# The conditioning vectors of a two-block network: column products on VectorE, ScalarE and GpSimd, and sums over partitions on TensorE

## The chip, the cores and the metric

The kernel runs on one core of a Trainium2 chip. A core has five engines with queues of their own: TensorE (matrix multiplication), VectorE, ScalarE, GpSimd, and SyncE, which here only issues DMAs. The metric is the device time of one execution in microseconds, the median of several runs.

## The reference

Two blocks are computed for a sequence x of 256 rows and 1024 columns, all in fp32. The first block has two layers of retention with stick-breaking attention and a gated feed-forward. The second block has two layers of feed-forward, mixer, feed-forward, for x and for a context of 256 rows. Its norms are modulated by nine vectors of 1024 in each layer, for x from c and for the context from c_ctx:

```python
sc, scc = jax.nn.silu(c), jax.nn.silu(c_ctx)
for l in range(DEPTH):                                   # 2
    mod_x = (sc @ w_mod[l] + b_mod[l]).reshape(b_, N_MOD, 1, D_MODEL)    # N_MOD = 9
    mod_h = (scc @ w_mod[l] + b_mod[l]).reshape(N_MOD, 1, D_MODEL)
    ...
# adaln_in:  rmsnorm(s, g_pre) * (1 + scale) + shift
# adaln_out: s + weight * gate * rmsnorm(y, g_post)
```

So w_mod is 2 x 1024 x 9216, 75 MB, and is multiplied by two vectors only. The last layer uses the context only up to its keys and values, so the last chunks of its w_mod are wanted for x alone.

## The kernel before

The work is a list of ten sub-layers, 0 to 9 (plan, SUBS): retention, feed-forward, retention, feed-forward of the first block, then feed-forward, mixer, feed-forward, twice. Each has a wide phase (input matrices, in chunks of 512 columns; a feed-forward has 11 chunks, each of 256 gate and 256 up columns) and a tall phase (output matrix). Weights come in units of 128x1024 fp32, 524 in all, over a ring of four slots (RING): SyncE loads raw, ScalarE rounds it to whi (split_hi, line 1102), VectorE takes the rest, wlo (split_lo, line 1663), and TensorE does three matmuls for each product (hi by hi, hi by lo, lo by hi). SyncE loads a unit when the unit four before it has been split; ScalarE copies a unit when the unit four before it has been used (unit_done of the trailing pass).

A wide chunk is four units. In the sub-layers with two row tiles (0 to 3 and 9) each unit holds 2 of the 8 blocks of the contraction; TensorE runs over the four units with the first tile (the leading pass) and then over the four with the second (the trailing pass), six matmuls a unit and pass. After the second unit of a leading pass it transposes hrow of the chunk before (gate_transposes for the trailing tile), after the second of a trailing pass that of the leading tile. VectorE's program for one chunk is: hrow of the chunk before, trailing tile; hrow of this chunk, leading tile; four splits for the next chunk. ScalarE's is sgate and hid for the tiles and the four copies, in the same order. With four row tiles (4 to 8), the chunks after the first of a feed-forward are computed transposed in one pass (wide_across), 24 matmuls a unit.

The modulation is laid between these passes by a plan made when the kernel is built (mod_plan). The 36 column chunks of w_mod make nine groups of four. A group has eight steps, one for each block of 128 rows (mod_step, inside the pe program): a load of 1 MB into mraw (two slots), and four matmuls of 512 columns, one for each chunk, whose stationary side is cstat, 32 columns of which the first two are silu(c) and silu(c_ctx); they lie in four column groups of the array and add up in PSUM bank 2. A step follows every second unit's trailing pass, in sub-layers 1, 3, 4, 6 (two groups each) and 7 (one). VectorE then copies the bank to mrow, TensorE turns it to columns with sel, and VectorE adds b_mod into modT.

GpSimd does the inverse roots, the rotary products and the DMAs of the gain rows (gain_rows, into grow). During the wide phases of the sub-layers with modulation it has nothing to do.

Of the kernel before, what the change touches and what calls it, by code (L numbers as in the profile page):

```python
# [152 lines left out]
def mod_plan():  # L153


    after, rows_at, cols_at = {}, {}, {}
    g = 0
    for i, groups in ((1, 2), (3, 2), (4, 2), (6, 2), (7, 1)):
        for j in range(groups):
            first = SUBS[i]["u_wide"] + 4 + 16 * j  # L160
            for k in range(KD):
                after[first + 2 * k] = KD * g + k
            rows_at[first + 14], cols_at[first + 18] = g, g
            g += 1
    return after, rows_at, cols_at


QUADS_AFTER, ROWS_AT, COLS_AT = mod_plan()
N_QUADS = len(QUADS_AFTER)
QUAD_UNIT = {q: u for u, q in QUADS_AFTER.items()}  # L170
assert N_QUADS == 2 * MOD_CHUNKS * DEPTH
N_Q4 = 48


def weight_units():
# [60 lines left out]
def build(nc, a, out):  # L236
    ctx = ExitStack()
    with ctx:  # L238
# [60 lines left out]
        r_row = region("grow", 8192)  # L299
        grow = at("grow", [P, 2, D], F32, r_row)  # L300
        rmask = at("rmask", [P, 4, 384], F32, r_row)
        cs1 = at("cs1", [P, 2, 2, P], F32, r_row + 6144)

        ident = sb("ident", [P, P])
# [10 lines left out]
        cT = sb("cT", [P, KD, 2])  # L315
        mrow = sb("mrow", [P, CH])
        sel = sb("sel", [P, 8])
        cstat = sb("cstat", [P, KD, 32])
# [42 lines left out]
        mraw_landed = [sem(f"mraw_landed{i}") for i in range(2)]  # L361
        ws_landed = sem("ws_landed")
        vgain_landed = sem("vgain_landed")
        out_landed = sem("out_landed")
# [2 lines left out]
        a_split = sem("a_split")  # L367
        w_split = sem("w_split")
        unit_done = sem("unit_done")
        mod_used = sem("mod_used")  # L370
        mod_rows = sem("mod_rows")
        mod_cols = sem("mod_cols")
        mod_taken = sem("mod_taken")
# [141 lines left out]
        @block.sync  # L515
        def _(sp):
            def load_main(u, slot, first=False):
                if not first:
                    sp.wait_ge(w_split, u - RING + 1)
                sp.dma_start(raw[:, slot, :], a["w"][WEIGHTS[u]]).then_inc(raw_landed[slot], 16)  # L520

            def load_mod(q):
                if q >= 2:
                    sp.wait_ge(mod_used, q - 1)
                g, k = q // KD, q % KD
                chunks = a["w_mod"].rearrange("(c u) p n -> c u p n", u=4)[4 * g:4 * g + 4, k // 2]
                src = chunks[:, :, CH * (k % 2):CH * (k % 2) + CH].rearrange("c p n -> p c n")
                sp.dma_start(mraw[:, q % 2, :, :], src).then_inc(mraw_landed[q % 2], 16)

            def load_mods(u):  # L530
                after_mix = SUBS[6]["u_wide"] + 4
                if u == after_mix:

                    sp.wait_ge(a_split, SUBS[6]["a0"])
                    load_mod(N_Q4)
                    load_mod(N_Q4 + 1)
                for q in range(2, N_QUADS):
                    if q not in (N_Q4, N_Q4 + 1) and QUAD_UNIT[q - 2] + 2 * RING == u:
                        load_mod(q)
# [12 lines left out]
            load_main(1, 1, first=True)  # L552
            load_x(1)
            load_main(2, 2, first=True)
            load_main(3, 3, first=True)
            for name, dst in (("cT", cT), ("lam", lamw), ("sink", sink)):
                constant(name, dst, small_landed, name != "cT")
            for u in range(RING, N_UNITS):
                load_main(u, u % RING)
                if u in LATE_AT:  # L560
                    name, dst = LATE_AT[u]
                    constant(name, dst, late_landed)
                if u in BLOCK2_AT:
# [4 lines left out]
                if u in (26, 27):  # L568
# [14 lines left out]
        def _(pe):  # L583
# [28 lines left out]
                        if i == nt - 1 and k % per == per - 1:  # L612
                            ins.then_inc(tr_ready, 1)

            def mod_step(q):
                g, k = q // KD, q % KD
                pe.wait_ge(mraw_landed[q % 2], 16 * (q // 2 + 1))
                if q == 0:
                    pe.wait_ge(c_split, 1)
                if k == 0 and g:  # L620
                    pe.wait_ge(mod_rows, g)
                for j in range(4):
                    last = mm(ps[32 * j:32 * j + 32, 2 * BANK:3 * BANK], cstat[:, k, :], mraw[:, q % 2, j, :],
                              k == 0, k == KD - 1)
                last.then_inc(mod_used, 1)

            def mod_columns(g):
                pe.wait_ge(mod_rows, g + 1)
# [4 lines left out]
                last.then_inc(mod_cols, 1)  # L633

            def modulation(u):
                if u in QUADS_AFTER:
                    mod_step(QUADS_AFTER[u])
                if u in COLS_AT:
                    mod_columns(COLS_AT[u])

# [447 lines left out]
        def _(act):  # L1088
# [563 lines left out]
        def _(dve):  # L1652
# [7 lines left out]
            def split_lo(u):  # L1660
                slot = u % RING
                dve.wait_ge(hi_done, u + 1)
                nc.vector.tensor_tensor(wlo[:, slot, :], raw[:, slot, :], whi[:, slot, :].bitcast(F32),  # L1663
                                        ALU.subtract).then_inc(w_split, 1)
                modulation(u - RING - 1)

            def mod_rows_out(g):
                dve.wait_ge(mod_used, KD * (g + 1))
# [12 lines left out]
                last.then_inc(mod_taken, 1)  # L1681

            def modulation(u):
                if u in ROWS_AT:
                    mod_rows_out(ROWS_AT[u])
                if u in COLS_AT:
                    mod_out(COLS_AT[u])

# [679 lines left out]


            dve.sem_inc(gate_done, LEAD4)  # L2370
            nc.vector.memset(cstat[:, :, :], 0.0).then_inc(dve_link, 1)
            n["link"] += 1
# [11 lines left out]
            nc.vector.tensor_copy(cstat[:, :, 0:2], cT[:, :, :])  # L2384
# [27 lines left out]
        def _(pool):  # L2412
# [16 lines left out]
            def gain_rows(s):  # L2429
# [16 lines left out]
                for st in range(streams):  # L2446
                    pool.dma_start(grow[:, st, :], gains[st].partition_broadcast(P)).then_inc(grow_ready, 16)

            def rope(view, cos, tmp, swap):

                t1, t2 = tmp
# [50 lines left out]
                inverse_roots(SUBS[0]["wide"][st])  # L2502
            for i, s in enumerate(SUBS):
                nxt = SUBS[i + 1] if i + 1 < len(SUBS) else None
                gain_rows(s)
                if s["kind"] == "ret":
                    rope_first(s)
                    for i0 in (8, 0):
                        inverse_roots_of_heads(i0, i0 + 8)
                if s["kind"] == "mix":  # L2510
                    pool.wait_ge(mod_used, N_Q4 if s["l"] == 0 else N_QUADS)
# [129 lines left out]
```

## Time and profile before

| | |
|---|---|
| time, median of 3 runs | 2510.45 us (2509.3 to 2510.86) |
| the profiled execution | 2511.7 us, span 2509.5 us |
| TensorE (PE) busy | 2418.1 us, 96% |
| VectorE (DVE) busy | 1144.3 us, 46% |
| ScalarE (ACT) busy | 1021.5 us, 41% |
| GpSimd (POOL) busy | 164.2 us, 7% |
| mean granted TensorE clock | 0.987 |
| moved by DMA | 364.34 MB, mean 145 GB/s |

The span runs from the first to the last instruction of the profiled execution; what its own time has beyond it lies before and after. Matmuls are pipelined and their ends are modelled, so that a difference of starts says what one costs, and the sum of durations does not. The times of sub-layer 1 (units 36 to 101) are about 140 to 360 us of the span, those of sub-layer 3 about 490 to 705, of sub-layer 9 from 2300 on.

### The profile page before, as it was taken

To read this page: it belongs to the slowest core of one execution; us is meant where nothing else is said; L and a number is where in the kernel's file an instruction comes from. 1 tells how busy PE (TensorE), PEld (TensorE's weight loads), DVE (VectorE), ACT (ScalarE), POOL (GpSimd) and SP (SyncE) were. 2 spreads that over 40 slices of the span, in tenths; PEclk is the share of its full clock that TensorE was granted. 3 is DMA by queue.
4 is the path that set the end of the run, shared out by engine and by line. 5 is a ranking of instruction groups with operands and counts; after the bars stand their busy time and mean duration, and the time that the engine had idled before them with its cause. 6 is when DMAs were issued, how large, how long until landed. Compare 5 with 4: busy or idle time off the path is not lost. (4 is left out here: it accounts for less than half of the span.)

```text
span 2509.5 us, 29213 instructions
## 1 busy us (share of the span) xinstructions
PE 2418.1 (96%) x11296; PEld 1902.9 (76%) x11296; DVE 1144.3 (46%) x1900; ACT 1021.5 (41%) x1766; POOL 164.2 (7%) x205
## 2 busy tenths in 40 slices
PE   8999999999999999999989999999999999997998
PEld 6776777766877778877677777887778887766777
DVE  5654455644552223363656222335323335456455
ACT  6443446543542222354545222234322234445444
POOL 1200003000010000013001000000000000310000
PEclk9999999999999999999989999999999999999999
DMA  6558654478545532323103554322442222322554
GB/s 212 188 185 293 236 175 164 138 261 292 194 138 185 175 134 91 103 69 125 43 26 109 193 176 168 109 85 92 161 142 93 100 86 92 115 70 76 181 187 143
DMA packets 118728, 364.34 MB, mean 145 GB/s; under 512 B 11072, under 2 KB 11712, under 8 KB 118592
## 3 DMA queue, kind: packets, MB, share of 16 engines
q1 hardware_dynamic: 116336, 355.62, 41.2%
q0 software_dynamic: 2256, 6.86, 0.9%
q8 instruction: 91, 1.49, 0.2%
q14 instruction: 45, 0.37, 0.1%
HBM read 361.35 MB, written 1.09 MB: 144 GB/s over the span
## 5 line engine op out<-in xcount | busy, mean ns | idle before, releaser
L1663 DVE TENSOR_TENSOR wlo<-raw,whi 128x1024 fp32r<-128x1024 f32 x524 | 644.2, 1234 | 732.4 <-ACT whi L1102 728.3
L1102 ACT CAST whi<-raw 128x1024 fp32r<-128x1024 f32 x524 | 548.2, 1050 | 618.2 <-PE ps L588 607.9
L588 PE MATMUL ps<-whi,xhi 128*128 128x512 f32 x1136 | 470.3, 414 | 25.9 <-ACT fbuf L1132 14.3
L588 PE MATMUL ps<-whi,xlo 128*128 128x512 f32 x1136 | 449.9, 396 | 0.0
L588 PE MATMUL ps<-wlo,xhi 128*128 128x512 f32 x1136 | 448.8, 395 | 0.0
L588 PE MATMUL ps<-whi,ahi 128*128 128x512 f32 x952 | 374.5, 393 | 7.6 <-DVE alo L1924 5.0
L588 PE MATMUL ps<-xhi,whi 128*128 128x512 f32 x960 | 378.9, 395 | 0.0
L588 PE MATMUL ps<-xhi,wlo 128*128 128x512 f32 x960 | 373.8, 389 | 0.0
L588 PE MATMUL ps<-xlo,whi 128*128 128x512 f32 x960 | 373.6, 389 | 0.0
L588 PE MATMUL ps<-whi,alo 128*128 128x512 f32 x952 | 371.8, 391 | 0.0
L588 PE MATMUL ps<-wlo,ahi 128*128 128x512 f32 x952 | 371.6, 390 | 0.0
L588 PEld LDWEIGHTS ps<-whi,xhi 128*128 128x128 f32 x1136 | 217.6, 192 | 99.3 <-issue 46.5
L588 PEld LDWEIGHTS ps<-whi,xlo 128*128 128x128 f32 x1136 | 216.7, 191 | 48.7
L588 PEld LDWEIGHTS ps<-wlo,xhi 128*128 128x128 f32 x1136 | 218.1, 192 | 39.3
L588 PEld LDWEIGHTS ps<-xhi,whi 128*128 128x128 f32 x960 | 180.2, 188 | 67.6 <-issue 31.9
L588 PEld LDWEIGHTS ps<-whi,ahi 128*128 128x128 f32 x952 | 179.4, 188 | 47.0 <-ACT proj L1330 4.8
L588 PEld LDWEIGHTS ps<-xhi,wlo 128*128 128x128 f32 x960 | 180.2, 188 | 38.3
L588 PEld LDWEIGHTS ps<-whi,alo 128*128 128x128 f32 x952 | 179.4, 188 | 37.9
L588 PEld LDWEIGHTS ps<-xlo,whi 128*128 128x128 f32 x960 | 180.3, 188 | 36.0
L588 PEld LDWEIGHTS ps<-wlo,ahi 128*128 128x128 f32 x952 | 179.7, 189 | 36.4
L1116 ACT CAST ahi<-hid 128x128 fp32r<-128x128 f32 (+1 forms) x264 | 86.4, 350 | 203.7 <-PE ps L588 203.6
L2423 POOL TENSOR_TENSOR rstd<-ms,mhalf 128x1 f32<-128x1 f32 (+1 forms) x55 | 38.7, 704 | 1946.4 <-DVE ms L1824 1319.5
(163 smaller groups left out, 1660.8 us busy)
## 6 DMA issues: line engine op xcount, KB each, us to landing
raw<-in_w SPq DMA_DIRECT2D x524, 512.0 KB, 3.4
mraw<-in_w_mod SPq DMA_DIRECT2D x72, 1024.0 KB, 6.6
grow<-gains POOLq DMA_DIRECT2D x11, 512.0 KB, 5.8
x<-in_x SPq DMA_DIRECT2D x2, 512.0 KB, 5.2
x<-in_ctx SPq DMA_DIRECT2D x1, 1024.0 KB, 7.7
out<-x SPq DMA_DIRECT2D x2, 512.0 KB, 2.6
rmask<-in_rmask SPq DMA_DIRECT2D x1, 768.0 KB, 5.2
ws<-in_ws POOLq DMA_DIRECT2D x2, 256.0 KB, 7.4
```

What stands on the lines that cost most here:

```text
L588: return nc.tensor.matmul(o, lhsT, rhs, start=start, stop=stop, skip_group_check=True)
L1102: nc.scalar.copy(whi[:, slot, :], raw[:, slot, :]).then_inc(hi_done, 1)
L1116: nc.scalar.copy(ahi[:, w * aslot:w * aslot + w], src[:, row, P * tiles[0]:P * tiles[0] + w]).then_inc(a_hi_done, 1)
L1663: nc.vector.tensor_tensor(wlo[:, slot, :], raw[:, slot, :], whi[:, slot, :].bitcast(F32), ALU.subtract).then_inc(w_split, 1)
L2423: nc.gpsimd.tensor_tensor(rstd[:, m0:m], ms[:, m0:m], mhalf[:, m0:m], ALU.pow).then_inc(rstd_ready, 1)
```

## The change

The modulation's products leave TensorE. A piece is now two column chunks of one block of rows (128 x 2 x 512, 0.5 MB), 144 in all; mraw has four slots of that size. A group is 16 pieces, one behind each of the 16 units from the seventh of its stretch on, and not one step behind every second unit.

- VectorE, for x: after split_lo(u) it multiplies the piece by silu(c), one value per partition, and adds it to macc in one scalar_tensor_tensor; the first piece of a half of a group is written by tensor_scalar.
- ScalarE, for the context, 112 of the 144: after split_hi(u) it multiplies the same piece by silu(c_ctx) with an activation, into msc1 or msc2 (two halves); the first two of a group go straight to macc.
- GpSimd, for the context: mod_group adds each scaled piece to macc, 14 for each of seven groups, 98 in all. The calls stand ahead of gain_rows in GpSimd's program.
- TensorE: mod_sum, once for each group, waits for all its pieces and additions and sums macc over the partitions, with a column of ones as the stationary side; 8 matmuls where there is a context part, else 4. It stands after the trailing pass of unit 18 (or 34) of the sub-layer; the group's last piece goes with unit 21 (37).
- SyncE loads a piece when the one four before it has been used by VectorE and ScalarE.

macc lies in rows, msc1 behind the operands of the first block, msc2 in grow. Copies to mrow, the turn to columns and modT are as they were.

```diff
-        for j in range(groups):
-            first = SUBS[i]["u_wide"] + 4 + 16 * j
-            for k in range(KD):
-                after[first + 2 * k] = KD * g + k
-            rows_at[first + 14], cols_at[first + 18] = g, g
+        for j in range(groups):
+            first = SUBS[i]["u_wide"] + 16 * j
+            pieces += [first + 6 + p for p in range(2 * KD)]
+            sum_at[first + 18], cols_at[first + 22] = g, g
...
+N_P4 = 96
+N_CTX = 112
...
-        mraw = at("mraw", [P, 2, 4, CH], F32, r_m)
+        mraw = at("mraw", [P, 4, 2, CH], F32, r_m)
+        macc = at("macc", [P, 2, 4, CH], F32, places["rows"])
...
+        ADDED = 2 * KD - 2
+        def scaled_pieces(s):
+            return msc1 if s["blk"] == 1 else msc2
...                                                        # sync
-            def load_mod(q):
-                if q >= 2:
-                    sp.wait_ge(mod_used, q - 1)
+            def load_mod(p):
+                if p >= 4:
+                    sp.wait_ge(mod_x, p - 3)
+                    sp.wait_ge(mod_scaled, min(p - 3, N_CTX))
...
+                    if p not in range(N_P4, N_P4 + 4) and PIECE_UNIT[p - 4] + RING + 2 == u:
+                        load_mod(p)
...                                                        # tensor
-            def mod_step(q):
-                g, k = q // KD, q % KD
-                pe.wait_ge(mraw_landed[q % 2], 16 * (q // 2 + 1))
...
-                for j in range(4):
-                    last = mm(ps[32 * j:32 * j + 32, 2 * BANK:3 * BANK], cstat[:, k, :], mraw[:, q % 2, j, :],
-                              k == 0, k == KD - 1)
-                last.then_inc(mod_used, 1)
+            def mod_sum(g):
+                parts = 2 if 2 * KD * g < N_CTX else 1
+                pe.wait_ge(mod_x, 2 * KD * (g + 1))
+                if parts == 2:
+                    pe.wait_ge(mod_ctx, ADDED * (g + 1))
...
+                for i in range(parts):
+                    for j in range(4):
+                        last = mm(ps[32 * j:32 * j + 32, 2 * BANK:3 * BANK], unit_col[:, i, :], macc[:, i, j, :],
+                                  i == 0, i == parts - 1)
+                last.then_inc(mod_summed, 1)
...                                                        # scalar, in split_hi(u)
+                if u in PIECE_AFTER:
+                    mod_piece(PIECE_AFTER[u], u)
+            def mod_piece(p, u):
+                if p >= N_CTX:
+                    return
+                s = [s for s in SUBS if s["u_wide"] <= u][-1]
+                g, k, half = p // (2 * KD), p % (2 * KD) // 2, p % 2
+                act.wait_ge(mraw_landed[p % 4], 16 * (p // 4 + 1))
+                act.wait_ge(c_silu, 1)
+                if k == 0:
+                    if g:
+                        act.wait_ge(mod_summed, g)
+                    dst = macc[:, 1, 2 * half:2 * half + 2, :]
+                else:
+                    if k >= 2:
+                        act.wait_ge(mod_ctx, ADDED * g + 2 * k - 3 + half)
+                    elif g:
+                        act.wait_ge(mod_ctx, ADDED * g)
+                    dst = scaled_pieces(s)[:, half, :, :]
+                nc.scalar.activation(dst, mraw[:, p % 4, :, :], ACT.Copy, scale=cT[:, k, 1:2]).then_inc(mod_scaled, 1)
...                                                        # vector, in split_lo(u)
+                if u in PIECE_AFTER:
+                    mod_piece(PIECE_AFTER[u])
+            def mod_piece(p):
+                g, k, half = p // (2 * KD), p % (2 * KD) // 2, p % 2
+                dve.wait_ge(mraw_landed[p % 4], 16 * (p // 4 + 1))
+                acc, piece = macc[:, 0, 2 * half:2 * half + 2, :], mraw[:, p % 4, :, :]
+                if k == 0:
+                    if g:
+                        dve.wait_ge(mod_summed, g)
+                    nc.vector.tensor_scalar(acc, piece, cT[:, k, 0:1], None, ALU.mult).then_inc(mod_x, 1)
+                else:
+                    dve.wait_ge(mod_x, p - 1)
+                    nc.vector.scalar_tensor_tensor(acc, piece, cT[:, k, 0:1], acc, ALU.mult, ALU.add).then_inc(mod_x, 1)
...                                                        # gpsimd, ahead of gain_rows(s)
+                for g in MOD_SUBS.get(i, ()):
+                    mod_group(s, g)
+            def mod_group(s, g):
+                if 2 * KD * g >= N_CTX:
+                    return
+                for p in range(2 * KD * g + 2, 2 * KD * (g + 1)):
+                    half = p % 2
+                    n["mod"] += 1
+                    pool.wait_ge(mod_scaled, p + 1)
+                    if p >= 2 * KD * g + 4:
+                        pool.wait_ge(mod_ctx, n["mod"] - 2)
+                    acc = macc[:, 1, 2 * half:2 * half + 2, :]
+                    nc.gpsimd.tensor_tensor(acc, acc, scaled_pieces(s)[:, half, :, :], ALU.add).then_inc(mod_ctx, 1)
+                pool.wait_ge(mod_ctx, n["mod"])
```

## Rows read from the trace of the kernel before

**Rows 1.** The page: busy time, share of the span, instructions.

```profile
PE 2418.1 (96%) x11296; PEld 1902.9 (76%) x11296; DVE 1144.3 (46%) x1900; ACT 1021.5 (41%) x1766; POOL 164.2 (7%) x205
```

**Rows 2.** Instructions with mraw: duration ns min/median/max, first and last start.

```profile
L588 PE MATMUL ps<-mraw,cstat x576: 592/605/617, 167.5 to 1864.5; 128*32 128x512 f32 x192
```

**Rows 3.** Timeline (start us, us, ...), TensorE, sub-layer 1, around a step.

```profile
164.72 0.39 PE L588 MATMUL ps<-whi,xhi 128*128 128x512 f32 x1
...
167.22 0.39 PE L588 MATMUL ps<-whi,xlo 128*128 128x512 f32 x1
167.53 1.06 PE L588 MATMUL ps<-mraw,cstat 128*32 128x512 f32 x8
168.53 0.50 PE L588 MATMUL ps<-whi,xhi 128*128 128x512 f32 x1
```

**Rows 4.** Timeline, ScalarE, sub-layer 9: first copies of two chunks.

```profile
2321.55 1.05 ACT L1102 CAST whi<-raw 128x1024 fp32r<-128x1024 f32 x1 [0.39 <-PE ps L588]
...
2333.20 1.05 ACT L1102 CAST whi<-raw 128x1024 fp32r<-128x1024 f32 x1 [0.98 <-PE ps L588]
```

**Rows 5.** Timeline, ScalarE, sub-layer 1: copies of units 40, 51 and 76.

```profile
155.94 1.05 ACT L1102 CAST whi<-raw 128x1024 fp32r<-128x1024 f32 x1 [0.89 <-PE ps L588]
...
188.58 1.05 ACT L1102 CAST whi<-raw 128x1024 fp32r<-128x1024 f32 x1 [1.55 <-PE ps L588]
...
283.13 1.06 ACT L1102 CAST whi<-raw 128x1024 fp32r<-128x1024 f32 x1 [0.88 <-PE ps L588]
```

**Rows 6.** Timeline, VectorE, sub-layer 1: the end of one burst.

```profile
189.67 1.23 DVE L1663 TENSOR_TENSOR wlo<-raw,whi 128x1024 fp32r<-128x1024 f32 x1 [1.38 <-ACT whi L1102]
190.81 0.47 DVE L1912 SCALAR_TENSOR_TENSOR hrow<-ps,rstd,sgate 128x256 f32<-128x256 f32 x1
```

**Rows 7.** Timeline, TensorE, at the same place.

```profile
190.90 0.39 PE L588 MATMUL ps<-whi,xlo 128*128 128x512 f32 x1
191.34 0.44 PE L647 MATMUL ps<-ident,hrow 128*128 128x128 f32 x2
```

**Rows 8.** Two lines of VectorE, columns as in rows 2.

```profile
L1832 DVE SCALAR_TENSOR_TENSOR x<-rows,rstd,x x20: 1276/1280/1286, 1089.3 to 2505.2; 128x1024 f32<-128x1024 f32 x20
L1704 DVE TENSOR_SCALAR rows<-x,rstd x22: 743/753/755, 705.5 to 2314.0; 128x1024 f32<-128x1024 f32 x22
```

**Rows 9.** Groups of ScalarE: count, busy us, mean ns, idle before, releasers.

```profile
L1197 ACT ACTIVATE rows<-x 128x1024 f32<-128x1024 f32 x32 | 33.9, 1059 | 45.1 <-DVE x L1804 24.4 <-DVE x L1832 16.6 <-DMA x<-in_x 2.4
...
L1285 ACT COPY hid<-ps 128x256 f32<-128x256 f32 x78 | 28.2, 370 | 95.9 <-PE ps L647 95.9
```

**Rows 10.** Timeline, GpSimd, sub-layer 0 (rotary products).

```profile
62.65 1.48 POOL L2456 TENSOR_TENSOR proj<-rope 128x512 f32<-128x512 f32 x1
67.06 1.56 POOL L2452 TENSOR_TENSOR rope<-proj,cs 128x512 f32<-128x512 f32 x1 [2.93 <-ACT proj L1330]
...
71.05 1.27 POOL L2456 TENSOR_TENSOR proj<-rope 128x512 f32<-128x512 f32 x1
...
73.87 1.42 POOL L2454 TENSOR_TENSOR rope<-proj,cs 128x256 f32<-128x256 f32 x2
```

**Rows 11.** Timeline, VectorE, sub-layer 0, at the same time.

```profile
62.91 2.30 DVE L1663 TENSOR_TENSOR wlo<-raw,whi 128x1024 fp32r<-128x1024 f32 x1
...
67.40 2.30 DVE L1663 TENSOR_TENSOR wlo<-raw,whi 128x1024 fp32r<-128x1024 f32 x1
...
69.63 1.01 DVE L2027 TENSOR_TENSOR zs<-zs,ps 128x384 f32<-128x384 f32 x2
```

**Rows 12.** Stretches: busy us (count) of PE, PEld, DVE, ACT, POOL; PEclk, DMA share, GB/s.

```profile
735.00:919.90 184.90, 184.90 (x865) 139.28 (x864) 50.29 (x53) 42.69 (x52) 1.10 (x2) 1.00 0.51 176
181.80:195.90 14.10, 14.05 (x72) 9.38 (x73) 5.78 (x6) 5.67 (x8) 0.00 (x0) 1.00 0.83 295
```

**Rows 13.** Timeline, TensorE, end of sub-layer 4, after idleness.

```profile
1107.13 0.47 PE L588 MATMUL ps<-whi,xhi 128*128 128x512 f32 x1 [3.28 <-ACT fbuf L1132]
```

**Rows 14.** A stretch there, columns as in rows 12.

```profile
1107.00:1112.00 5.00, 4.87 (x14) 3.87 (x15) 5.00 (x9) 2.26 (x6) 1.25 (x1) 0.66 0.47 156
```

More of the change, by code:

```diff
@@ L153, in mod_plan @@
 def mod_plan():
-    after, rows_at, cols_at = {}, {}, {}
+    subs, pieces, sum_at, cols_at = {}, [], {}, {}
     g = 0
     for i, groups in ((1, 2), (3, 2), (4, 2), (6, 2), (7, 1)):
+        subs[i] = range(g, g + groups)
         for j in range(groups):
-            first = SUBS[i]["u_wide"] + 4 + 16 * j
-            for k in range(KD):
-                after[first + 2 * k] = KD * g + k
-            rows_at[first + 14], cols_at[first + 18] = g, g
+            first = SUBS[i]["u_wide"] + 16 * j
+            pieces += [first + 6 + p for p in range(2 * KD)]
+            sum_at[first + 18], cols_at[first + 22] = g, g
             g += 1
[L165 to L172, printed above, removed]
+    return subs, pieces, sum_at, cols_at
+MOD_SUBS, PIECE_UNIT, SUM_AT, COLS_AT = mod_plan()
+N_PIECES = len(PIECE_UNIT)
+PIECE_AFTER = {u: p for p, u in enumerate(PIECE_UNIT)}
+assert N_PIECES == 4 * MOD_CHUNKS * DEPTH == len(PIECE_AFTER)
+N_P4 = 96
+N_CTX = 112
 def weight_units():
@@ L301, in build @@
         rmask = at("rmask", [P, 4, 384], F32, r_row)
+        msc1 = at("msc1", [P, 2, 2, CH], F32, r_x + 16384)
+        msc2 = at("msc2", [P, 2, 2, CH], F32, r_row)
         cs1 = at("cs1", [P, 2, 2, P], F32, r_row + 6144)
@@ L317, in build @@
         sel = sb("sel", [P, 8])
-        cstat = sb("cstat", [P, KD, 32])
+        unit_col = sb("unit_col", [P, 2, 32])
         modT = sb("modT", [P, DEPTH, N_MOD * KD, 2])
@@ L360, in build @@
         raw_landed = [sem(f"raw_landed{i}") for i in range(RING)]
-        mraw_landed = [sem(f"mraw_landed{i}") for i in range(2)]
+        mraw_landed = [sem(f"mraw_landed{i}") for i in range(4)]
         ws_landed = sem("ws_landed")
@@ L369, in build @@
         unit_done = sem("unit_done")
-        mod_used = sem("mod_used")
+        mod_x = sem("mod_x")
+        mod_scaled = sem("mod_scaled")
+        mod_ctx = sem("mod_ctx")
+        mod_summed = sem("mod_summed")
         mod_rows = sem("mod_rows")
@@ L520, in load_main @@
                 sp.dma_start(raw[:, slot, :], a["w"][WEIGHTS[u]]).then_inc(raw_landed[slot], 16)
-            def load_mod(q):
-                if q >= 2:
-                    sp.wait_ge(mod_used, q - 1)
-                g, k = q // KD, q % KD
-                chunks = a["w_mod"].rearrange("(c u) p n -> c u p n", u=4)[4 * g:4 * g + 4, k // 2]
+            def load_mod(p):
[3 more added lines that the diff above has]
+                g, k, half = p // (2 * KD), p % (2 * KD) // 2, p % 2
+                c0 = 4 * g + 2 * half
+                chunks = a["w_mod"].rearrange("(c u) p n -> c u p n", u=4)[c0:c0 + 2, k // 2]
                 src = chunks[:, :, CH * (k % 2):CH * (k % 2) + CH].rearrange("c p n -> p c n")
-                sp.dma_start(mraw[:, q % 2, :, :], src).then_inc(mraw_landed[q % 2], 16)
+                sp.dma_start(mraw[:, p % 4, :, :], src).then_inc(mraw_landed[p % 4], 16)
             def load_mods(u):
-                after_mix = SUBS[6]["u_wide"] + 4
-                if u == after_mix:
+                if u == SUBS[6]["u_wide"] + 4:
                     sp.wait_ge(a_split, SUBS[6]["a0"])
[L535 to L539, printed above, removed]
+                    for p in range(N_P4, N_P4 + 4):
+                        load_mod(p)
+                for p in range(4, N_PIECES):
+                    if p not in range(N_P4, N_P4 + 4) and PIECE_UNIT[p - 4] + RING + 2 == u:
+                        load_mod(p)
             def constant(name, dst, sem_, broadcast=False):
@@ L567, in _ @@
                     sp.dma_start(x[:, 2:4, :], a["ctx"].rearrange("b (t p) d -> p (b t) d", p=P)).then_inc(block2_landed, 16)
-                if u in (26, 27):
+                if u in (26, 27, 28, 29):
                     load_mod(u - 26)
@@ L613, in transposes_in @@
                             ins.then_inc(tr_ready, 1)
-            def mod_step(q):
-                g, k = q // KD, q % KD
-                pe.wait_ge(mraw_landed[q % 2], 16 * (q // 2 + 1))
-                if q == 0:
+            def mod_sum(g):
[3 more added lines that the diff above has]
+                    pe.wait_ge(mod_ctx, ADDED * (g + 1))
+                if g == 0:
                     pe.wait_ge(c_split, 1)
-                if k == 0 and g:
+                else:
                     pe.wait_ge(mod_rows, g)
-                for j in range(4):
-                    last = mm(ps[32 * j:32 * j + 32, 2 * BANK:3 * BANK], cstat[:, k, :], mraw[:, q % 2, j, :],
-                              k == 0, k == KD - 1)
-                last.then_inc(mod_used, 1)
+                for i in range(parts):
[3 more added lines that the diff above has]
+                last.then_inc(mod_summed, 1)
             def mod_columns(g):
@@ L635, in modulation @@
             def modulation(u):
-                if u in QUADS_AFTER:
-                    mod_step(QUADS_AFTER[u])
+                if u in SUM_AT:
+                    mod_sum(SUM_AT[u])
                 if u in COLS_AT:
@@ L1665, in split_lo @@
                 modulation(u - RING - 1)
+                if u in PIECE_AFTER:
+                    mod_piece(PIECE_AFTER[u])
+            def mod_piece(p):
+                g, k, half = p // (2 * KD), p % (2 * KD) // 2, p % 2
+                dve.wait_ge(mraw_landed[p % 4], 16 * (p // 4 + 1))
[4 more added lines that the diff above has]
+                    nc.vector.tensor_scalar(acc, piece, cT[:, k, 0:1], None, ALU.mult).then_inc(mod_x, 1)
+                else:
+                    dve.wait_ge(mod_x, p - 1)
+                    nc.vector.scalar_tensor_tensor(acc, piece, cT[:, k, 0:1], acc, ALU.mult, ALU.add).then_inc(mod_x, 1)
             def mod_rows_out(g):
-                dve.wait_ge(mod_used, KD * (g + 1))
+                dve.wait_ge(mod_summed, g + 1)
                 if g:
@@ L1683, in modulation @@
             def modulation(u):
-                if u in ROWS_AT:
-                    mod_rows_out(ROWS_AT[u])
+                if u in SUM_AT:
+                    mod_rows_out(SUM_AT[u])
                 if u in COLS_AT:
@@ L2370, in _ @@
             dve.sem_inc(gate_done, LEAD4)
-            nc.vector.memset(cstat[:, :, :], 0.0).then_inc(dve_link, 1)
-            n["link"] += 1
+            link(nc.vector.memset(unit_col[:, :, :], 0.0))
+            for i in range(2):
+                nc.vector.memset(unit_col[:, i, i:i + 1], 1.0)
             nc.vector.memset(ones[:, :], 1.0)
@@ L2383, in _ @@
             dve.wait_ge(c_silu, 1)
-            nc.vector.tensor_copy(cstat[:, :, 0:2], cT[:, :, :])
             nc.vector.tensor_copy(sel[:, :].rearrange("p (j t) -> p j t", j=4),
@@ L2510, in _ @@
                 if s["kind"] == "mix":
-                    pool.wait_ge(mod_used, N_Q4 if s["l"] == 0 else N_QUADS)
+                    pool.wait_ge(mod_x, N_P4 if s["l"] == 0 else N_PIECES)
                     pool.dma_start(ws[:, :, :], a["ws"][s["l"]]).then_inc(ws_landed, 16)
```

## The prediction

> **What bounds the kernel now.** I read the page first. TensorE is busy in 96% of the span of 2509.5 us [rows 1], and the chain of waits is nearly all its matmuls. So a microsecond leaves the total only where TensorE itself gets it back, and a microsecond on another engine counts where TensorE comes to wait for it. Next I asked for the instructions that read mraw, and for TensorE's timeline around one of them: what does the modulation cost TensorE? Then the chunk cycle of a two-tile gate/up phase (sub-layers 1, 3 and 9), by ScalarE's, VectorE's and TensorE's timelines: how much room have the two engines that the change loads? Last, all places where VectorE and GpSimd work at once.
>
> Modulation today: 576 records of 605 ns [rows 2], 8 to a step, 72 steps, overlapping. In the timeline the last matmul of the unit starts at 167.22 and the next unit's first at 168.53 [rows 3]. From 164.72 on, matmuls of weights start 0.227 us apart (eleven steps to 167.22), so a step costs 1.31 - 0.23 = 1.08 us of TensorE, and 72 steps 78 us.
>
> **Two-tile chunk cycle (sub-layers 1 and 3).** A ring slot is held from the leading to the trailing pass. A pass of one unit is 6 x 0.227 = 1.36 us. ScalarE may copy a unit of the next chunk when the trailing pass of the same-numbered unit of this one ends. From first copy to first copy a chunk takes 2333.20 - 2321.55 = 11.65 us in sub-layer 9, which has no modulation [rows 4]. In sub-layer 1 the nine chunks from 155.94 to 283.13 take 127.2 us [rows 5]; sub-layer 3 is the same stretch again. The rows to look at are the end of the burst. VectorE's program is: four splits, then hrow of the chunk before (trailing tile). TensorE wants that hrow after the *second* leading pass. Slot 3 comes free at 188.58 [rows 5], its split runs 189.67 to 190.90, hrow 190.81 to 191.28 [rows 6], and TensorE, done with the second leading pass, transposes hrow at 191.34 [rows 7]. There is no slack: whatever is put on VectorE between the splits and hrow delays TensorE.
>
> **Part 1, matmuls out, sums in.** Out: 72 x 1.08 = 78. In: seven groups sum two parts and two groups one, 16 sums of the form of a step, 16 x 1.08 = 17. TensorE's own gain is 61 us. Column sums, copies of rows and modT stay.
>
> **Part 2, VectorE.** One piece of 128x1024 behind each of 144 splits. The nearest rows are a scalar_tensor_tensor of that size at 1.28 and, for the first of a group, tensor_scalar at 0.75 [rows 8]; queued behind each other some 0.08 is hidden, as between split and hrow [rows 6]. **ScalarE** gets 112 scalings, near the 1.05 of its copy [rows 5]; other 1024-wide activations take 1.06 [rows 9].
>
> **Part 3, GpSimd.** 98 additions of 128x1024. The trace has 512 wide at 1.27 and two of 256 at 1.42, so 0.71 each [rows 10]: slope 2.19 ns per element, 1.27 + 512 x 0.00219 = 2.39 us. Bounds: 2.2 (slope alone) and 2 x 1.56 = 3.1 (from the longest row shown). By the Trainium skill (GPSIMD Engine Reference, Elementwise — side-by-side cycle accounting) a two-input add of 2048 takes 4497 ns; half is, as an estimate, 2.25, which would take 0.14 off each of the 56 additions that count below, 8 us.
>
> **Part 4, what the two do to each other.** GpSimd's 512-wide multiplication at 62.65 ends at 64.13, and VectorE's split, issued at 62.91, takes 2.30 instead of 1.23: 1.22 of waiting and 1.08 of work. The same at 67.06 (ends 68.62) and 67.40 [rows 10, 11]. At 69.63 two operations with one input in PSUM and one in SBUF take 1.01, no longer than usual, beside GpSimd [rows 11]. So operations with two SBUF inputs take turns with GpSimd, whole instructions at a time, and both the split and the new piece are of that kind. The Trainium skill (SBUF — State Buffer, SBUF: two separate sides) calls it an exclusive lock on a port pair and gives it to whichever starts first, for the whole instruction; it promises no turns, and by it alone VectorE could keep the pair through its queue, which is rival A. In turns VectorE holds it 1.08 and GpSimd about 2.28 (2.39 less what it dispatches meanwhile; for 512 it would be 64.13 - 62.99 = 1.14).
>
> *Full chunk* (four pieces, four additions; six of them in each of sub-layers 1 and 3). Time 0 is the first copy. ScalarE: copy 0 to 1.05, scale 2.1, copy 3.15, scale 4.2, then hid 0.37 [rows 9], copy 5.6, scale 6.65, copy 7.7, scale 8.9. From 1.1 on there is always something to add, so the holders are four splits, four pieces and four additions: 8 x 1.08 + 4 x 2.28 = 17.8, done at 19.0. hrow to 19.5, transposes to 19.95, third and fourth leading pass 2.72, trailing pass 1.36: 24.05 us instead of 11.65.
> *Chunk 1*: its pieces 6 and 7 open a group (0.75 each, no addition): two such behind the last two splits, 13.2.
> *Chunks 5 and 9*, where a group is summed: TensorE asks for the sum after the third trailing pass (4.1), but needs the pieces and additions of units whose slots came free at 0 and 1.36: 1.1 + 4 x 1.08 + 2 x 2.28 = 10.0. Sum 2.15, to 12.2; fourth trailing pass 13.6; only now the last copy, split, row copy 0.68, piece and hrow, 17.6; transposes, two leading passes and one trailing: 22.1, in chunk 9 (no pieces for 38 and 39) 21.5.
> Nine chunks: 13.2 + 6 x 24.05 + 22.1 + 21.5 = 201.1 against 127.2: +73.9, in both sub-layers **+148**.
>
> *Four-tile sub-layers 4, 6, 7.* 32 units take 184.9 us with modulation, 5.78 each, 5.45 the 24 matmuls alone; VectorE is busy 50.3 of it, 1.57 a unit [rows 12], and with a piece and a wait for an addition gets 1.08 + 2.28 more: 4.9. A unit may be copied four units ahead. The cover holds. TensorE gets back 40 x 1.08 - 8 x 1.08 = 34.6; at each of the three sums with additions it waits some 0.3 to 0.5 (copy, split, addition and piece after one another take 5.8 of the 5.45 it has). **-33**.
>
> *TensorE's clock.* In a full chunk TensorE now idles some 9 us before hrow. After 3.28 us of idleness it restarts at 1107.13 [rows 13], and in 1107 to 1112 the granted clock is 0.66, part at 1.2 instead of 2.4 GHz [rows 14]: 5 x 0.34 = 1.7 us lost. The passes behind hrow are on the path. Sixteen chunks (all but the first of each nine): **+27**. Bounds: nothing, and all 4.1 us of the exposed passes at half clock, 66 us.
>
> SP: pieces of half the size, one a unit, the same bytes. Share of the DMA engines in such a chunk was 0.83 at 14.1 us [rows 12]; at 24 it falls. GpSimd's gain_rows now queue behind the additions, but they serve the end of the tall phase, over 100 us later: nothing, and if that cover went, one wait of some us. VectorE's and ScalarE's waits of a group's first piece for the sum are in chunk 5.
>
> **Sum.** +148 - 33 + 27 = +142. The profiled run took 2511.7, which gives 2653; the median of the runs is 1.2 below it, so 2652.
>
> **Rivals.**
> *A. GpSimd finds gaps, additions drop behind.* It may fall two behind and catch up while TensorE does the 4.5 us behind hrow; two additions a chunk leave the path: 24.05 - 4.6 = 19.5. With no clock loss: 13.2 + 6 x 19.5 + 20 + 19.4 = 169.6, +42 per sub-layer, total 2511.7 + 85 - 33 = 2563. For it: two of three holders are VectorE's, and its queue is never empty. Against: both engines waited for at most one instruction, so turns are fair.
> *B. No turns with these operations (the other side).* Place: the burst before hrow in sub-layers 1 and 3. Then VectorE does eight operations at 1.15 in a row behind a copy: 10.3, hrow, transposes and three passes: 15.2 a chunk. Summing chunks: TensorE waits for scale and addition, till 6.6: 17.7 and 17.3. Nine chunks: 13.2 + 91.2 + 35.0 = 139.4, +12.2; twice that less 33 is -9: 2503, faster. It decides once a full chunk is below 16.6 us (12 x 1.4 = 16.7 lost more pays for the rest). Against it the two splits of 2.30.
> *C. VectorE's pieces hide altogether*: 2512 - 61 = 2451. This would need slack before hrow, and [rows 5 to 7] show none.
> *D. Half clock for longer, additions near 2.6*: 16 x 2.4 + 56 x 0.3 = +55, 2708. Behind 9 us of idleness no row shows how long half clock lasts.
>
> **Chances.** Forecast 0.65 (own range 2600 to 2690), A 0.14, D 0.11, B 0.07, C 0.03. Slower 0.89; from B and C 0.08 faster, 0.03 between. A difference under 0.2% (5 us) can't be told from no change. The range, 2555 to 2710, leaves out the far side of D and B and C.
>
> **What would show it.** In the profile after: splits of sub-layer 1 at 2.3 to 3.5 us in place of 1.23; additions at 2.4 or, when waiting, 3.5; ten us idle of TensorE's weight load put down to hrow of line 1912 (renumbered), twelve times and more; TensorE busy well below 9 tenths in the slices of sub-layers 1 and 3; a chunk cycle of 24 us there, and units 0.5 us shorter in 4 and 6. Wrong if additions run beside undisturbed splits (B), if the cycle is 20 (A), or if TensorE waits in sub-layers 4 and 6, where I see cover.

## The result, and the profile after

| | before | after |
|---|---|---|
| median | 2510.07 us (4 runs) | 2668.68 us (2667.55 to 2669.68, 4 runs) |
| ratio, 95% interval | | 1.0628 [1.0615, 1.0641] |
| profiled execution, span | 2511.7, 2509.5 us | 2668.23, 2666.4 us |
| mean granted TensorE clock | 0.987 | 0.951 |

The change makes the kernel 6.3% slower, 159 us. The forecast was 2652, with a range of 2555 to 2710.

The page after, against [rows 1]. First busy time, then three of the rows of 40 slices (tenths; TensorE, GpSimd, TensorE's granted clock), then groups (busy us, mean ns, idle before).

```profile
PE 2401.1 (90%) x10848; PEld 1929.5 (72%) x10848; DVE 1509.2 (57%) x2045; ACT 1137.8 (43%) x1878; POOL 426.9 (16%) x303
...
PE   8975679996559999999999999999999999998998
...
POOL 1123410303440043200211023000100000310000
PEclk9987789997779999999999999999999999999999
...
L1707 DVE TENSOR_TENSOR wlo<-raw,whi 128x1024 fp32r<-128x1024 f32 x524 | 685.4, 1312 | 539.8 <-ACT whi L1123 535.3
...
L2519 POOL TENSOR_TENSOR macc<-macc,msc 128x1024 f32<-128x1024 f32 x98 | 263.0, 2691 | 448.5 <-ACT msc L1146 448.5
L1724 DVE SCALAR_TENSOR_TENSOR macc<-mraw,cT,macc 128x1024 f32<-128x1024 f32 x126 | 326.6, 2592 | 1.5 <-DMA mraw<-in_w_mod 1.5
```

TensorE's busy time barely falls and its share drops from 96% to 90%. The loss has a place: slices 3 to 6 and 10 to 12, sub-layers 1 and 3, and there the clock falls as well. The new operation of VectorE takes 2.59 us on average where one of its size takes 1.28 [rows 8]; half of it is waiting that the profile counts as busy.

Lengths of the wide phases, from the first copy of the phase to the first of the tall phase (us), and the nine chunks of [rows 5]:

| | before | after | |
|---|---|---|---|
| sub-layer 1 | 156.4 | 246.9 | +90.5 |
| sub-layer 3 | 154.9 | 250.5 | +95.6 |
| sub-layer 4 | 260.8 | 250.6 | -10.2 |
| sub-layer 6 | 256.1 | 246.6 | -9.5 |
| sub-layer 7 | 245.5 | 236.9 | -8.6 |
| nine chunks, sub-layer 1 / 3 | 127.2 / 127.2 | 217.6 / 217.7 | +90.4 / +90.5 |

The sum, +157.8, is the span's difference of 156.9. Six chunks of each nine take 25.4 to 26.8 us, the two with a sum 24.2 and 23.5.

One full chunk, VectorE's timeline (start, us) from its first split to hrow; the first copy started at 271.77.

```profile
272.86 1.22 DVE L1707 TENSOR_TENSOR wlo<-raw,whi 128x1024 fp32r<-128x1024 f32 x1 [1.46 <-ACT whi L1123]
274.00 3.49 DVE L1724 SCALAR_TENSOR_TENSOR macc<-mraw,cT,macc 128x1024 f32<-128x1024 f32 x1
277.41 3.38 DVE L1707 TENSOR_TENSOR wlo<-raw,whi 128x1024 fp32r<-128x1024 f32 x1
280.72 3.40 DVE L1724 SCALAR_TENSOR_TENSOR macc<-mraw,cT,macc 128x1024 f32<-128x1024 f32 x1
284.04 1.21 DVE L1707 TENSOR_TENSOR wlo<-raw,whi 128x1024 fp32r<-128x1024 f32 x1
285.17 1.27 DVE L1724 SCALAR_TENSOR_TENSOR macc<-mraw,cT,macc 128x1024 f32<-128x1024 f32 x1
286.37 1.21 DVE L1707 TENSOR_TENSOR wlo<-raw,whi 128x1024 fp32r<-128x1024 f32 x1
287.50 0.37 DVE L1738 TENSOR_TENSOR modT<-ps,bmod 128x8 f32<-128x8 f32 x4
287.80 3.06 DVE L1724 SCALAR_TENSOR_TENSOR macc<-mraw,cT,macc 128x1024 f32<-128x1024 f32 x1
290.78 0.47 DVE L1971 SCALAR_TENSOR_TENSOR hrow<-ps,rstd,sgate 128x256 f32<-128x256 f32 x1
```

GpSimd's additions at that time.

```profile
274.02 5.69 POOL L2519 TENSOR_TENSOR macc<-macc,msc 128x1024 f32<-128x1024 f32 x2 [18.63 <-ACT msc L1146]
280.55 2.49 POOL L2519 TENSOR_TENSOR macc<-macc,msc 128x1024 f32<-128x1024 f32 x1 [0.84 <-ACT msc L1146]
286.74 3.04 POOL L2519 TENSOR_TENSOR macc<-macc,msc 128x1024 f32<-128x1024 f32 x1 [3.71 <-ACT msc L1146]
```

Each of the four additions has one operation of VectorE that is 1.8 to 2.2 us too long, and from first copy to the end of hrow, 291.25, it is 19.5 us, as the prediction had it. (The "x2" are two additions merged by the view.) Then TensorE (timeline), and its clock from there to the next first copy (a stretch, columns as in [rows 12]).

```profile
291.31 0.69 PE L668 MATMUL ps<-ident,hrow 128*128 128x128 f32 x2 [8.63 <-DVE hrow L1971]
```

```profile
291.30:298.00 6.70, 6.69 (x21) 5.45 (x22) 0.48 (x1) 0.85 (x2) 0.00 (x0) 0.66 0.13 48
```

TensorE stood 8.63 us for hrow, and the passes behind it take 6.7 instead of 4.5 us at a mean clock of 0.66, as in [rows 14].

### The profile page after: what moved, and what is told of

The parts are those of the page before. It is cut to its first block and busy times, and to the rows that moved or that the text cites. A ratio compares the mean times of both kernels' runs of the same rounds, so it can differ in the third digit from the quotient of the medians.

```text
span 2666.4 us, 29225 instructions
## 1 busy us (share of the span) xinstructions
PE 2401.1 (90%) x10848; PEld 1929.5 (72%) x10848; DVE 1509.2 (57%) x2045; ACT 1137.8 (43%) x1878; POOL 426.9 (16%) x303
## 5 line engine op out<-in xcount | busy, mean ns | idle before, releaser
L1707 DVE TENSOR_TENSOR wlo<-raw,whi 128x1024 fp32r<-128x1024 f32 x524 | 685.4, 1312 | 539.8 <-ACT whi L1123 535.3
L605 PE MATMUL ps<-whi,xhi 128*128 128x512 f32 x1136 | 484.5, 427 | 64.1 <-DVE wlo L1707 38.5
L605 PE MATMUL ps<-whi,xlo 128*128 128x512 f32 x1136 | 462.7, 407 | 0.0
L605 PE MATMUL ps<-wlo,xhi 128*128 128x512 f32 x1136 | 461.7, 406 | 0.0
L2519 POOL TENSOR_TENSOR macc<-macc,msc 128x1024 f32<-128x1024 f32 x98 | 263.0, 2691 | 448.5 <-ACT msc L1146 448.5
L1724 DVE SCALAR_TENSOR_TENSOR macc<-mraw,cT,macc 128x1024 f32<-128x1024 f32 x126 | 326.6, 2592 | 1.5 <-DMA mraw<-in_w_mod 1.5
L605 PEld LDWEIGHTS ps<-whi,xhi 128*128 128x128 f32 x1136 | 227.2, 200 | 127.0 <-DVE wlo L1707 45.9
L605 PEld LDWEIGHTS ps<-whi,xlo 128*128 128x128 f32 x1136 | 224.6, 198 | 51.6
L605 PEld LDWEIGHTS ps<-wlo,xhi 128*128 128x128 f32 x1136 | 227.2, 200 | 42.1
```

Of the source, the lines that this page charges most:

```text
L605: return nc.tensor.matmul(o, lhsT, rhs, start=start, stop=stop, skip_group_check=True)
L1724: nc.vector.scalar_tensor_tensor(acc, piece, cT[:, k, 0:1], acc, ALU.mult, ALU.add).then_inc(mod_x, 1)
L2519: nc.gpsimd.tensor_tensor(acc, acc, scaled_pieces(s)[:, half, :, :], ALU.add).then_inc(mod_ctx, 1)
```

## The experiments

In all that leave the additions out, ScalarE still scales and all waits but those for the additions stay. "Two-tile" means sub-layers 1 and 3.

**e1_no_additions.** In mod_group:

```diff
-                    nc.gpsimd.tensor_tensor(acc, acc, scaled_pieces(s)[:, half, :, :], ALU.add).then_inc(mod_ctx, 1)
+                pool.wait_ge(mod_scaled, 2 * KD * (g + 1))
```

> The changed kernel without GpSimd's 98 additions (so the context's sums hold only their first pieces); ScalarE still scales all 112 pieces, VectorE's pieces are unchanged. Theory 1 (splits and pieces take turns with the additions, four of 2.28 us in a full chunk of sub-layers 1 and 3): a full chunk falls from 26.4 us to the 15.2 of eight VectorE operations in a row, perhaps 16 with some half clock; the kernel takes 2500 to 2515 us, level with the one before. Theory 2 (VectorE's queue alone makes the delay, the additions run beside it): nothing to gain, 2669 us.

Measured: 2564.71 us, 1.0212 [1.0194, 1.0230]. The additions cost 104 us, so theory 2 falls; but a full chunk takes 20.2 us and not 15 to 16, and 50 us are unexplained. ScalarE's timeline has the cause, with its releaser:

```profile
254.30 1.05 ACT L1123 CAST whi<-raw 128x1024 fp32r<-128x1024 f32 x1
257.91 1.15 ACT L1142 ACTIVATE msc<-mraw,cT 128x1024 f32<-128x1024 f32 x1 [2.56 <-DMA mraw<-in_w_mod]
258.96 1.03 ACT L1123 CAST whi<-raw 128x1024 fp32r<-128x1024 f32 x1
261.22 1.15 ACT L1142 ACTIVATE msc<-mraw,cT 128x1024 f32<-128x1024 f32 x1 [1.23 <-DMA mraw<-in_w_mod]
```

**e2_half_additions.** The additions' views cover one chunk of columns instead of two.

> Each of GpSimd's additions covers 512 of its 1024 columns (half of the context's additions left out), their number and waits unchanged. Theory 1: an addition holds VectorE up for its whole length, now 1.14 instead of 2.28 us, so a full chunk falls by 4 x 1.14 = 4.6 to 21.9 us; twelve such chunks and four with two additions give 12 x 4.6 + 4 x 2.3 = 64 us: 2605 us. Rival (what costs is the handing over between the two, the same for each instruction): 2665 us, chunk 26.

Measured: 2582.76 us (one run), full chunks 20.4 to 21.7. The cost goes with the length, so it isn't the handing over; but it fell by more than half of e1's gain, in a kernel whose pieces still came late. Repeated as e6.

**e3_filled.** In TensorE's program:

```diff
+            def fill(times):
+                for _ in range(times):
+                    mm(bank(7, 0, P), ident[:, :], ones[:, :], True, True)
...
                         elif c:
+                            if filled(s, c):
+                                fill(28)
                             gate_transposes(s, c - 1, TRAIL)
```

> The changed kernel, with matmuls of 128 columns of constants into an unused bank where TensorE idles in sub-layers 1 and 3: 10 ahead of the second leading pass, 28 ahead of the transposes of hrow, in the six full chunks, and 28 ahead of the four sums. Theory (part of the loss is TensorE's half clock after these waits, in passes that lie on the path): the granted clock of these stretches goes from about 0.7 to nearly 1.0, a full chunk from 26.4 to about 24.2, and the kernel from 2669 to 2630 to 2645 us. Rival (the passes at half clock are hidden in the next wait): 2665 to 2675 us whatever the clock.

Measured: 2642.39 us, 1.0526 [1.0504, 1.0548]: 26 us less with more work on TensorE. Same stretch of sub-layer 1, the changed kernel, then this one:

```profile
170.00:250.00 80.00, 46.10 (x164) 35.16 (x163) 57.79 (x32) 30.55 (x38) 34.11 (x13) 0.77 0.44 158
```

```profile
170.00:250.00 80.00, 67.97 (x447) 59.24 (x446) 62.09 (x34) 30.83 (x38) 36.55 (x13) 1.00 0.50 177
```

In the three full chunks of this stretch, where the clock stays at 1.00, a chunk is 24.1 us, which is the 24.05 of the prediction without its clock term; in the next three it still fell (0.93 on average) and they take 25.5 to 25.7. So half clock behind hrow is on the path: the same three chunks take 26.4, 26.8 and 25.4 in the changed kernel, 2.1 us more on average.

**e4_steps_first.** Groups 0 to 3 by mod_step, with cstat, as before; the rest as after.

```diff
-            pieces += [first + 6 + p for p in range(2 * KD)]
+            if g < STEP_GROUPS:                              # 4
+                for k in range(KD):
+                    steps[KD * g + k] = first + 4 + 2 * k
+            else:
+                pieces += [first + 6 + p for p in range(2 * KD)]
```

> Groups 0 to 3 (sub-layers 1 and 3) by matmuls of every step, as before; groups 4 to 8 (sub-layers 4, 6, 7) as in the changed kernel. Theory 1 (all of the loss lies in the two-tile sub-layers, the four-tile ones gained 28 us): 2478 to 2485 us, faster than both. Rival (the two-tile sub-layers also lose elsewhere, by the shared loads or by what follows): 2500 us or more.

Measured: 2480.40 us, 0.9881 [0.9864, 0.9897]. The nine two-tile chunks are back at 127.2 us. All of the loss lay in the two-tile sub-layers, and the rest of the change is a gain of 30 us.

**e5_no_additions_early.** e1, and:

```diff
-                    if p not in range(N_P4, N_P4 + 4) and PIECE_UNIT[p - 4] + RING + 2 == u:
+                    if p not in range(N_P4, N_P4 + 4) and PIECE_UNIT[p - 4] + RING == u:
```

> e1_no_additions again (GpSimd's additions left out), but SyncE issues the load of a piece two units earlier, right behind the one whose slot it takes. In e1_no_additions a full chunk took 20.2 us and not 15.2; in its timeline ScalarE stands from 255.4 to 257.9 and 260.0 to 261.2 before it scales the third and fourth piece. Theory (these loads are issued only after the first and second split of the same burst, and land too late): chunk 15.2 to 17 us, kernel 2500 to 2525 us. Rival (half clock or a longer VectorE queue makes the rest): chunk 20, 2560 us.

Measured: 2521.30 us, 1.0047 [1.0032, 1.0062], chunk 17.1. The late loads were worth 43 us in e1. What is left is twelve microseconds over the kernel before, although TensorE's own gain is in it: the price of VectorE's pieces between the splits, with the half clock behind them. Its timeline has VectorE's eight operations in a row, none waiting, ahead of hrow (the last four shown; the mark stands for modT):

```profile
240.93 1.22 DVE L1703 TENSOR_TENSOR wlo<-raw,whi 128x1024 fp32r<-128x1024 f32 x1
242.06 1.28 DVE L1720 SCALAR_TENSOR_TENSOR macc<-mraw,cT,macc 128x1024 f32<-128x1024 f32 x1
243.26 1.22 DVE L1703 TENSOR_TENSOR wlo<-raw,whi 128x1024 fp32r<-128x1024 f32 x1
...
244.69 1.27 DVE L1720 SCALAR_TENSOR_TENSOR macc<-mraw,cT,macc 128x1024 f32<-128x1024 f32 x1
```

**e6_half_early.** e2 with that load line.

> e2_half_additions (additions of 512 of 1024 columns) with the early loads of e5_no_additions_early. Theory (turns, once the loads are out of the way): the burst is 1.1 + 8 x 1.08 + 4 x 1.14 = 14.3 us, the chunk 19.3 at full clock, up to 21 with half clock; between e5 and e7 in even steps. Rival (late loads only moved the additions about): below e5 plus 2 us.

Measured: 2594.38 us (one run), full chunks 21.1 to 22.6.

**e7_early.** The changed kernel with that load line.

> The changed kernel with the early loads and nothing else. Theory (with full additions VectorE and GpSimd fill the burst by turns, so a late piece is hidden): 2655 to 2675 us, chunk 25.5 to 26.5. Rival (late loads cost here too, as in e1_no_additions): 4 us a chunk less, 2610 us.

Measured: 2666.25 us, 1.0628 [1.0611, 1.0646]. With early loads and none, half and full additions the times are 2521, 2594 and 2666: 73 and 72 us, even steps (the middle one is a single run). In e6's timeline a held operation is 1.1 us too long, against 2.2 in the changed kernel:

```profile
279.73 1.23 DVE L1707 TENSOR_TENSOR wlo<-raw,whi 128x1024 fp32r<-128x1024 f32 x1 [1.47 <-ACT whi L1123]
280.87 2.33 DVE L1724 SCALAR_TENSOR_TENSOR macc<-mraw,cT,macc 128x1024 f32<-128x1024 f32 x1
283.12 2.31 DVE L1707 TENSOR_TENSOR wlo<-raw,whi 128x1024 fp32r<-128x1024 f32 x1
```

The late loads cost nothing by themselves in the changed kernel, where VectorE's queue is full by turns anyway. Why e2, with late loads, is 12 us *faster* than e6 was not tried; each is one run.

**e8_two_later.** e4, with `first` two units later in sub-layers 4 and 6.

> e4_steps_first, with the pieces of sub-layers 4 and 6 two units later (sums and columns too). In e4_steps_first TensorE stands 3.4 us in the third chunk of each until VectorE has written hid, which is behind a burst of splits, pieces and additions where the four-tile phase begins. Theory: this stall and a half-clock stretch behind it go, 3.4 to 5 us in each: 2470 to 2475 us. Rival (the stall moves with the pieces): 2480 us.

Measured: 2474.14 us, 0.9857 [0.9842, 0.9871]. TensorE's waits between 690 and 960 us, e4 and then e8 (total, times, longest):

```profile
PE ps L619 <- DVE hid L2049: 3.4, 1, 3.4
```

```profile
PE ps L619 <- DVE macc L1754: 1.6, 2, 0.8
```

The wait for hid, which the changed kernel has too (3.4 us in each of the two sub-layers), is gone; that for the sums grows from 0.6 to 1.6. The time is 6 us less, and the two intervals overlap a little.

**e9_no_gpsimd.** e8, and for groups 4 to 6 on VectorE, with nothing on ScalarE and GpSimd:

```diff
+                    for i, acc in enumerate(accs):
+                        last = nc.vector.scalar_tensor_tensor(acc, piece, cT[:, k, i:i + 1], acc, ALU.mult, ALU.add)
+                    last.then_inc(mod_x, 1)
```

> e8_two_later, with the context's products too on VectorE (a second tensor_scalar or scalar_tensor_tensor behind each piece of groups 4 to 6); nothing on ScalarE and GpSimd. Theory: in a four-tile unit VectorE then needs 1.57 + 2 x 1.20 = 4.0 of 5.45 us and never waits for GpSimd; TensorE's waits at the sums (0.3 us) stay: 2469 to 2475 us, equal to e8 within 3 us. Rival (VectorE gets too full at the start of the four-tile phase): 2480 us.

Measured: 2469.16 us, 0.9837 [0.9824, 0.9851], the best of all that compute everything; the two intervals overlap, so "not slower than e8" is what it shows. In its trace the wait for the sums is gone from that stretch.

**e10_behind_early.** e7 with the sums of sub-layers 1 and 3 two units later, and there on VectorE (ScalarE likewise, behind silus):

```diff
                     if c and ffn:
                         gates(s, c - 1, TRAIL)
+                        for u in range(4 * c, 4 * c + 4):
+                            if s["u_wide"] + u in PIECE_AFTER and behind(s["u_wide"] + u):
+                                mod_piece(PIECE_AFTER[s["u_wide"] + u])
```

> e7_early, with the pieces of sub-layers 1 and 3 on VectorE and ScalarE behind hrow and sgate of the trailing tile instead of between the splits (sums and columns two units later). Theory (what costs is what stands ahead of hrow, and the turns as far as they must be paid somewhere): splits and hrow run free, and the chunk falls to what VectorE and GpSimd need by turns, 17.8 us plus hrow and hand-overs, 18.5 to 20: 12 x 7 = 84 us less, 2575 to 2600 us. Rival (the place does not matter): 2660 us.

Measured: 2598.64 us, 1.0357 [1.0342, 1.0371]: 68 us less than e7, by the place of the pieces (and of the sums). Full chunks take 21.1 to 22.2 us, more than the 18.5 to 20 expected. What e11 shows of SyncE's queue may be part of that; the loads of e12 were not tried with the additions in.

**e11_behind_early_no_add.** e10 without the additions.

> e10_behind_early without GpSimd's additions (left out of the result). Theory: VectorE has 4 x 2.4 + 1.0 = 10.6 us of work in a chunk of 11.65 and the pieces fill its idle time: chunk 11.7 to 13, all of TensorE's own 61 us gained but for the sums' waits: 2455 to 2475 us. Rival (VectorE's pieces cost by themselves wherever they stand): as e5_no_additions_early, 2520 us.

Measured: 2503.07 us, 0.9971 [0.9962, 0.9981]; 28 us above what was expected. Timeline of SyncE, and of ScalarE:

```profile
177.16 0.38 SPq L553 DMA_DIRECT2D mraw<-in_w_mod  x1
179.30 0.33 SPq L542 DMA_DIRECT2D raw<-in_w  x1
189.44 0.38 SPq L553 DMA_DIRECT2D mraw<-in_w_mod  x1
```

```profile
181.97 1.05 ACT L1130 CAST whi<-raw 128x1024 fp32r<-128x1024 f32 x1 [1.65 <-DMA raw<-in_w]
185.53 1.04 ACT L1130 CAST whi<-raw 128x1024 fp32r<-128x1024 f32 x1 [2.50 <-DMA raw<-in_w]
```

SyncE stands at a piece's load until VectorE has used the slot, which is now behind hrow, and the weight loads stand behind it. So against e5 the new place, with the later sums, gained 18 us.

**e12_behind_loads_last.** e11, and for the two-tile pieces `load_unit(p)` is the last unit of the piece's own chunk.

> e11_behind_early_no_add again (pieces of sub-layers 1 and 3 behind hrow, GpSimd's additions left out), but SyncE issues the piece loads of a chunk behind all four weight loads of the same chunk. In e11 SyncE stood at a piece's load, whose slot comes free only behind hrow, with the next weight load queued behind it: no load between 179.3 and 189.4, and ScalarE waited 1.7 and 2.5 us for raw. Theory (that queue was what spoilt e11; VectorE's own pieces fit into its idle time behind hrow): a chunk 11.7 to 13 us, kernel 2455 to 2475 us. Rival (the pieces cost wherever they stand): 2500 us as in e11.

Measured: 2451.80 us, 0.9776 [0.9758, 0.9793]. Thirteen of the eighteen chunks take 11.3 to 12.0 us, as if without modulation; the two behind which the first group of a sub-layer is summed take 16.4, the other three 12.6 to 12.8. VectorE, where a piece follows hrow at once:

```profile
205.42 1.23 DVE L1719 TENSOR_TENSOR wlo<-raw,whi 128x1024 fp32r<-128x1024 f32 x1 [0.16 <-ACT whi L1136]
206.56 0.48 DVE L1983 SCALAR_TENSOR_TENSOR hrow<-ps,rstd,sgate 128x256 f32<-128x256 f32 x1
206.95 2.47 DVE L1736 SCALAR_TENSOR_TENSOR macc<-mraw,cT,macc 128x1024 f32<-128x1024 f32 x2
```

It leaves the context's additions out and so is no version to use; it prices VectorE's part alone.

## Why the prediction was right

The time is 16 us above the forecast: 6 of them are the nine chunks with their clock, in both two-tile sub-layers together, 5 the rest of sub-layer 3, 5 the four-tile sub-layers.

*Slack ahead of hrow: none.* Shown. Ahead of hrow the pieces cost 70 us more (e5, 2521) than behind it with the loads put last (e12, 2452), and there most chunks are as long as without modulation. The place alone is not the whole of the 70: with the loads in e5's order it gave 18 (e11), and 51 came when the queue that it had spoilt was mended.

*Turns with GpSimd.* Shown, by dose: 145 us for 98 additions with early loads, 72.5 for each half. The 17.8 us of holding were right in sum, in part by luck: in the chunk shown, by differences of starts, four splits take 1.14 and four pieces 1.20 each (9.4, where 8.6 was worked out), the waits are 2.21, 2.17, 2.12 and 1.78 (8.3, for 9.1), and the write of modT, which was left out, adds 0.3. An undisturbed addition takes 2.36 to 2.41, for 2.39 from the slope of [rows 10]. Rival A falls: the additions don't slip into gaps. So does the reading, cited there, that VectorE could keep the port pair: while an addition waited, it gave the pair up after each operation. Nor do the additions act by way of ScalarE, which waits for them before it writes msc again: in e7 those waits are 8.7 us in all, and in the chunk shown VectorE's operations follow each other without idle time, only longer.

*Full chunk.* 24.05 without the clock and 25.75 with it; 24.1 in e3, 26.2 in the chunk shown.

*Clock.* Right in kind, small in size: the term was 1.7 for each of 16 chunks, 27 us. A full chunk loses 2.1 on average in the three of e3, 2.2 in the one shown. Nine chunks and clock together were +175 in the two sub-layers and are +181. Sub-layer 3 loses another 5 outside these nine: 1.6 in its first chunk and 3.5 in its last, where ScalarE waits 3.1 us for a weight load. Why they come late was not tried.

*Sums at chunks 5 and 9.* 22.1 and 21.5 and 1.7 of clock each; 24.2 and 23.5 measured.

*Four-tile sub-layers.* -33, measured -28. The step that failed is "the cover holds": at the start of the four-tile phase three units are copied in a burst, VectorE, held by additions, writes hid late, and TensorE stands 3.4 us in sub-layers 4 and 6. VectorE (the lines between are left out) and TensorE in the changed kernel:

```profile
941.64 3.44 DVE L1724 SCALAR_TENSOR_TENSOR macc<-mraw,cT,macc 128x1024 f32<-128x1024 f32 x1
945.00 3.42 DVE L1707 TENSOR_TENSOR wlo<-raw,whi 128x1024 fp32r<-128x1024 f32 x1
948.35 3.41 DVE L1724 SCALAR_TENSOR_TENSOR macc<-mraw,cT,macc 128x1024 f32<-128x1024 f32 x1
...
954.02 1.27 DVE L2016 TENSOR_TENSOR hid<-pgate,ps 128x512 f32<-128x512 f32 x2
```

```profile
954.74 0.79 PE L605 MATMUL ps<-xhi,whi 128*128 128x512 f32 x1 [3.42 <-DVE hid L2016]
```

In the traces of e8 and e9 this wait is gone.

*SP.* "One a unit, the same bytes" overlooked that a piece's load is issued only behind the split two units before it, which in a burst is too short: in e1 the third piece's load went out at 252.82, ScalarE wanted it at 255.35, and it landed by 257.91. ScalarE waits 82.3 us in all for mraw after the change. e7 shows that this costs nothing there; e1 and e5 show that it would have cost 43 us as soon as the turns were gone. So rival B's time was too short: without the additions the changed kernel takes 2565, with early loads 2521, and 2503 was the forecast of neither. Most of the other 18 is half clock, which rival B left out: in e5 a chunk is 17.1 where 15.2 was worked out, and in the one from 199.98 to 217.11 what lies behind hrow takes 6.2 us instead of 4.5.

*Rival C*, 2451, is near e12's 2452, partly by luck. The gain of 61 is 58 from median to median, in a kernel without the additions whose two first sums each still cost 4.7 us; against that its eighteen two-tile chunks gained 31.5 us, where 32 steps at 1.08 less the sums make 26. Between the changed kernel and this time stood the additions, the place of the pieces and the order of the loads.

## What to carry to other kernels

Before work is moved to an engine with idle time, look at which of its instructions the bound engine waits for, and what stands ahead of it in the program: here idle time behind that instruction was nearly free (e12), idle time ahead of it was not (e5). GpSimd was no spare engine beside a VectorE with a full queue of operations with two inputs in SBUF: each addition of 2.4 us added some 2.2 us to that queue. Where VectorE had room, in the four-tile sub-layers, the additions cost little (e8 and e9 are 5 us apart, and their intervals overlap). And a load that waits for a slot must not stand ahead of the loads that the bound engine lives on.

## What the runs showed of the hardware

VectorE operations with two SBUF inputs and GpSimd's additions alternated instruction by instruction: while both had work queued, neither got two in a row in the stretches shown; a VectorE operation of 1.2 to 1.3 us then took 3.3 to 3.5 beside an addition of 128x1024 and 2.3 beside one of 128x512. An activation with a scale from SBUF, 128x1024, takes 1.15 us where a copy of that size takes 1.05. TensorE idled 7.5 to 8.8 us before hrow in the full chunks of sub-layer 1; after one of these stretches, of 8.63 us, the mean granted clock was 0.66 over 6.7 us. With matmuls of no use in the idle time it stayed at 1.00 in three of the six, was 0.93 over the other three, and the kernel took 26 us less.
